# A routed-expert loop on one core: the slot look-up moved between the transposes and the down products, and the residual added in mid-loop

## The reference

```python
comb = (one_hot(expert_id, 32) * weight[..., None]).sum(1)   # top 2 experts of each token
out = zeros((256, 1024))
for e in range(32):
    hg, hu = split(t @ w_gate_up[e], 2)                       # w_gate_up[e]: 1024 x 512
    out = out + comb[:, e:e+1] * ((silu(hg) * hu) @ w_down[e]) # w_down[e]: 256 x 1024
x = layer_norm(alpha * x + out, ln2_g, ln2_b)                 # alpha = 2 ** 0.25
```

## Time and profile before

| what | value |
|---|---|
| time, median of 3 runs | 559.55 us (557.23 to 559.96) |
| the profiled execution: its span | 555.2 us (the profile gives no other time of this execution) |
| median less span | 4.35 us |
| TensorE busy | 499.0 us, 90% of the span |
| VectorE, ScalarE busy | 284.6 us, 168.1 us |
| HBM read | 143.60 MB |

### The profile page before, as it was taken

The page is one execution under the profiler, slowest core; times in us unless marked ns, Lnnn a source line. Parts: engine busy times, 40 slices in busy tenths (PEclk is TensorE's granted clock), DMA queues, the critical chain, the costliest instruction groups (busy, mean ns, idle before and its releaser), DMA issues.

```text
span 555.2 us, 7508 instructions
## 1 busy us (share of the span) xinstructions
PE 499.0 (90%) x2754; PEld 345.5 (62%) x2754; DVE 284.6 (51%) x559; ACT 168.1 (30%) x332; POOL 24.1 (4%) x39
## 2 busy tenths in 40 slices
PE   5999999998999998999559899999999999999981
PEld 4999999987999895887456364333333333333430
DVE  2489898597789996664745122122222222222116
ACT  3432322457554438343322121111111111111111
POOL 2000000000000000000000001000011111111000
PEclk9999999999999999999757999999999999999996
DMA  7668874424244442357911685999999999999802
GB/s 288 228 266 317 335 269 152 152 76 152 92 175 148 156 152 77 113 168 307 421 50 67 250 344 192 421 418 420 421 423 423 421 422 421 422 423 421 368 1 77
DMA packets 26365, 145.05 MB, mean 261 GB/s; under 512 B 3040, under 2 KB 3296, under 8 KB 13792
## 3 DMA queue, kind: packets, MB, share of 16 engines
q1 hardware_dynamic: 26336, 144.66, 67.0%
HBM read 143.60 MB, written 1.05 MB: 261 GB/s over the span
## 4 chain that ended last, share of the span: by engine, by line
PE 76%; DVE 15%; ACT 5%; issue 2%; DMA 1%; ACTq 0%; SPq 0%; DVEq 0%
PE bank L1258 20%; PE bank L1277 11%; PE bank L1067 10%; PE bank L1045 7%; PE bank L1047 6%; PE bank L1046 6%; DVE slots L679 5%; PE bank L1290 3%; DVE w_lo L665 3%; PE bank L1291 3%; PE bank L1233 2%; ACT w_hi L438 1%; PE bank L1188 1%; PE bank L1109 1%; ACT kT L599 1%
## 5 line engine op out<-in xcount | busy, mean ns | idle before, releaser
L1258 PE MATMUL bank<-slots,raw 128*64 128x512 f32 x496 | 113.4, 595 | 0.0
L679 DVE SCALAR_TENSOR_TENSOR slots<-slots,par 128x256 f32<-128x256 f32 x240 | 98.3, 477 | 0.2
L1045 PE MATMUL bank<-x_hi,w_hi 128*128 128x256 f32 x304 | 90.4, 297 | 7.7 <-DVE w_lo L665 4.8
L1046 PE MATMUL bank<-x_lo,w_hi 128*128 128x256 f32 x304 | 86.0, 283 | 0.0
L1047 PE MATMUL bank<-x_hi,w_lo 128*128 128x256 f32 x304 | 85.9, 283 | 0.0
L665 DVE TENSOR_TENSOR w_lo<-raw,w_hi 128x1024 fp32r<-128x1024 f32 x54 | 66.0, 1222 | 38.5 <-ACT w_hi L438 38.5
L438 ACT CAST w_hi<-raw 128x1024 fp32r<-128x1024 f32 x54 | 56.6, 1047 | 57.7 <-PE bank L1047 51.3
L1067 PE MATMUL bank<-gates,raw 128*128 128x256 f32 x288 | 67.9, 391 | 6.7 <-DMA raw<-in_w_in 6.7
L1258 PEld LDWEIGHTS bank<-slots,raw 128*64 128x64 f32 x496 | 35.2, 137 | 60.7 <-issue 60.3
L1277 PE MATMUL bank<-slots,kT 128*64 128x512 f32 x256 | 58.5, 598 | 12.0 <-ACT kT L599 12.0
L983 DVE SCALAR_TENSOR_TENSOR pT<-pT,kT,bank 128x256 f32<-128x256 f32 x16 | 7.7, 480 | 112.2 <-ACT pT L593 112.2
(11 more groups left out here) (181 smaller groups left out, 542.2 us busy)
## 6 DMA issues: line engine op xcount, KB each, us to landing
slots<-in_w_gate_up SPq DMA_DIRECT2D x62, 1024.0 KB, 12.5
slots<-in_w_down SPq DMA_DIRECT2D x32, 1024.0 KB, 14.3
raw<-in_w_in SPq DMA_DIRECT2D x48, 512.0 KB, 4.5
raw<-in_w_attn SPq DMA_DIRECT2D x8, 512.0 KB, 3.4
raw<-in_w_conv SPq DMA_DIRECT2D x8, 512.0 KB, 3.4
raw<-in_w_out SPq DMA_DIRECT2D x8, 512.0 KB, 3.4
spare<-in_w_gate_up SPq DMA_DIRECT2D x2, 1024.0 KB, 11.5
gates<-in_xT SPq DMA_DIRECT2D x2, 512.0 KB, 5.4
```

Of the source, the lines that this page charges most:

```text
L679: ins = nc.vector.scalar_tensor_tensor(acc[:, i, :], h_pad[:, i, tap:tap + SEQ], w, acc[:, i, :], ALU.mult, ALU.add)
L1045: mm(dst, ah, bh, start=first, stop=False, **kw)
L1046: mm(dst, ah, bl, start=False, stop=False, **kw)
L1258: ins = mm(gu_bank[j * WIN:(j + 1) * WIN, :], xg[u][:, k, j * WIN:(j + 1) * WIN], w, start=(k == 0), stop=(k == KT - 1))
```

## The change

The look-up for the next pair stands between the transposes and the down products, and writes into `gu_bank` (bank 0) for every pair but the first. `gate_up` now waits until ScalarE has copied token and weight out of that bank. The look-up does not wait for `hT_copied` any more. ScalarE copies token and weight ahead of `split_y_hi`. The loop of TensorE is cut in two (pairs 4 to 7 and pairs 8 to 13), with `residual` between them in place of its old position in the last pair.

```diff
+        def info_bank(p):
+
+            return turn_bank if is_pair(p, 0) else gu_bank
@@ copy_info, ScalarE
-                nc.scalar.copy(token[u], turn_bank[:, 0:1])
+                nc.scalar.copy(token[u], info_bank(p)[:, 0:1])
                 for j in range(2):
                     ins = nc.scalar.copy(weight[u][j * WIN:(j + 1) * WIN, :],
-                                         turn_bank[j * WIN:(j + 1) * WIN, 1 + j:2 + j])
+                                         info_bank(p)[j * WIN:(j + 1) * WIN, 1 + j:2 + j])
@@ pair, ScalarE
                 copy_hT(p)
-                split_y_hi(p)
                 if not last:
                     copy_info(p + 1, 1 - u)
+                split_y_hi(p)
@@ slot_info, TensorE
                 pe.wait_ge(gat_built, p + 1)
-                if from_pair(p, 1):
-                    pe.wait_ge(hT_copied, p)
                 for t in range(TT):
-                    ins = mm(turn_bank[:, 0:3], gat[u][:, t, :], info[u][:, t, :], start=(t == 0), stop=(t == TT - 1))
+                    ins = mm(info_bank(p)[:, 0:3], gat[u][:, t, :], info[u][:, t, :], start=(t == 0), stop=(t == TT - 1))
@@ gate_up, TensorE
                     pe.wait_ge(h_ready, p)
+                    pe.wait_ge(info_copied, p + 1)
@@ pair, TensorE
                 if last:
-                    residual(first=False)
                     scatter(p - 1, 1 - u)
...
                 turn_h(p)
+                if not last:
+                    slot_info(p + 1, 1 - u)
                 for j in range(2):
                     pe.wait_ge(wd_loaded[2 * u + j], 16 * turn)
                 down(p, (2 * u, 2 * u + 1))
-                if not last:
-                    slot_info(p + 1, 1 - u)
@@ the loop, TensorE
-            with pe.Fori(2, PAIRS // 2 - 1) as i:
+            with pe.Fori(2, PAIRS // 4) as i:
+                for u in range(2):
+                    pair(i * 2 + u, u, i + 1)
+            residual(first=False)
+            with pe.Fori(PAIRS // 4, PAIRS // 2 - 1) as i:
                 for u in range(2):
                     pair(i * 2 + u, u, i + 1)
```

## The result

The changed kernel took 548.82 us (median of 4 runs, 548.18 to 549.83) against 559.33 us for the kernel before (4 runs, 557.23 to 559.96). The ratio is 0.983, with a 95% interval from 0.9805 to 0.9855. The forecast was 552.6 us, with a range down to 550.8.

A forecast was written before the change was run, and what follows sets the result against it. TensorE's order was taken to bound the loop, with the weights close behind. Look-up -8.1 + 0.3, residual 0, lost cover +0.75 and weights +0.15 gave -6.9 us: 559.55 to 552.6 us, range 550.8 to 556.5.

The forecast's parts named there:

- The bound: Expert loop: TensorE's order sets the time; the weights' lead is down to 2.6 us at pair 14.
- The look-up: Gap between transposes and down products hides it: 15 times 0.54 leave the chain, -8.1 us, with +0.3 us remaining.
- The residual: Moved from ahead of pair 15 to between pairs 7 and 8: -3.54 and +3.54 us; the queue does not run dry.
- The lost cover: Tail, `scatter(14)`: the split behind `down(14)` is no longer covered by the residual, 2.6 - 1.85 = +0.75 us.
- The weights: Landings come 1.04 us earlier; `gate_up(14)` waits 0.14 us for its third piece, written +0.15, bounds 0 and 1.2.
- The sum: All terms of the change together: -6.9 us, made against the span of 555.2, which becomes 548.3.
- From span to median: Outside the span: the median lies 4.35 us above it and nothing there changes, so 559.55 - 6.9 = 552.65 us.
- A: `gate_up(14)`: weights set the time, landings do not move forward, wait 1.2 us, 553.7 us in all; chance 0.14.
- B: Gap before down products does not hide the look-up: 556.2 us if half hidden, 560.3 if not at all; chance 0.11.
- C: Entry of TensorE's second loop: instruction fetch queues behind the weights, 11.1 us, giving 563.7 us, slower; chance 0.05.

The follow-up runs named there:

- The look-up alone: Changed kernel with the residual put back ahead of pair 15, so only the look-up moves, against the kernel before: 553.68 us, ratio 0.9929.
- its lighter version: Look-up moved, residual ahead of pair 15, only an eighth of each expert's down weights loaded from pair 2 on, against the kernel before: 547.49 us, ratio 0.9811.

## Why the prediction was right and wrong

**The bound.** Right. TensorE's order set the loop, and the weights were met at pair 14, as said, as the only wait. The look-up alone and its lighter version show both halves of that.

**The look-up.** Right in kind, too small in size. From `gate_up(0)` to `gate_up(15)` the steps of the two traces, less the residual, the uncovered split and the wait, are 9.85 us shorter for 15 look-ups, 0.66 each, where the sum had 0.52. The gap did hide it: it grew in two pairs only, by 0.03 us in pair 6 and 0.16 in pair 7, and in the trace of the look-up alone it did not grow in these two. The sum had allowed 0.3 for this. The rest comes from `gate_up`, which is 0.15 us shorter directly behind the down products than behind the look-up, 13 times over (15 x 0.54 + 13 x 0.15 - 0.2 = 9.85). In the changed kernel it is again 7.02 behind the residual. Down and gate products use half the columns of the array each (64), and look-up, residual and scatter all 128, so a change of shape seems to cost 0.15 us. The first weight loads of `gate_up` in the trace of after speak for it, behind the down products and behind the residual:

```profile
391.00 0.15 PEld L1261 LDWEIGHTS bank<-slots,raw 128*64 128x64 f32 x2 [0.28 <-issue]
...
422.47 0.20 PEld L1261 LDWEIGHTS bank<-slots,raw 128*64 128x64 f32 x4 [0.76 <-issue]
```

In the first place the loads start 0.60 us ahead of the products at 391.60, and in the second only 0.07 ahead of those at 422.54, so there the load is not covered by the products before it. No run changed the shape alone, so the cause stays argued.

**The residual.** Right. It took 3.63 us in mid-loop and 3.54 in the tail. The lost cover is 2.58 us from the end of `down(14)` to `gate_up(15)`, against 1.85 for the scatter before: 0.73, forecast 0.75.

**The weights.** The wait was sized 0.15 and is 1.03 us, since TensorE came earlier than thought. Measured from `gate_up(0)` on, the third piece of pair 14 lands 2.2 us earlier than before, not 1.04. Of that 1.39 is the earlier issue at 344.21. The other 0.8 us I cannot place.

**The sum.** -9.85 + 0.09 + 0.73 + 1.03 = -8.0 us inside the expert part, against -6.9. `gate_up(0)` started 0.76 us later in the one trace of after, and 0.1 more lies behind `gate_up(15)`. So the span came out 7.1 us shorter, at nearly the predicted value, by luck: the loop gained 1.1 more, and the trace of after began 0.76 later. Inside the 1.1 two misses go against each other as well, the look-ups with 2.05 us more gain and the wait for weights with 0.88 more loss.

**From span to median.** This is the step that failed: "The median of the runs lies 4.35 above the span, and nothing in what lies around the span changes". A run lies 1.7 to 1.9 us above its own span. The 4.35 compared the span of one execution with the time of another. The profiled execution, at 555.2, belongs to a time near 557, the shorter group. Two of the three runs shown lie at 559.55 and 559.96, the longer group, and so does the median. What the longer group adds was taken for a constant and carried over, which put the forecast about 2.6 us too high. That alone takes it to 550.0 us, already outside the range, whose bounds had no term for it. The other 1.1 us down to the measured 548.82 are the loop's greater gain. The four first runs of the changed kernel all fell into its shorter group, and the difference of the medians became 10.5 us. On a chip where both kernels were run in turn the changed kernel takes 7.3 us less (549.1 to 551.0 us by the interval). The -6.9 of the sum lies inside that, but within either group the difference is 7.6 to 7.7, nearer to the -8.0 of the traces. Why one set of runs falls mostly into one group stays open.

**The rivals.** By the sign that the prediction named, a wait of over 1 us, A would be called right: `gate_up(14)` is 1.03 us longer (the row of the wait has 0.9). A gave the right place of the wait, but its premise, landings that do not move, is wrong: they moved by 2.2 us. So that sign did not tell A from the forecast. B falls by the gap in the trace. C falls: at `gate_up(8)`, the entry of the second loop, there is no gap, and the 0.16 us ahead of `down(7)` are missing in the second trace of the changed kernel. The Trainium skill's rule on taken branches ("Runtime: NRT & Kernel Launch", section "Instruction fetch mechanics") shows no cost at this entry in this trace. The signs by which the prediction was to fail, a pair over 14 us or a span over 552, both stayed away: none of them looked at the step from span to median.

## What to carry to other kernels

Small work that TensorE does between large products is free in a gap in which TensorE waits for another engine's copy, if it reads nothing that the copy makes and is over before the copy and its hand-over are. Where TensorE's order and the weights run close together, filler work belongs ahead of the point at which the weights are met, since behind it the same work is paid in full. Before a span is turned into a time, each run's own span has to be set beside its time, and if the runs fall into groups, the forecast has to say from which group it starts.

## What the runs showed of the hardware that I had not expected

- The granted clock made two groups of runs of one and the same kernel, 2.3 us apart in the traces. In the longer group it fell once more at 312 us (0.59 over the next 3 us), which cost 1.3 us, after TensorE had been busy 1.15 of 3 us. In another trace TensorE was busy 1.06 of those 3 us and the clock did not fall.
- The clock differed ahead of that too: it rose from its half level between 299 and 302 us early or late (0.96 or 0.70 over that stretch), and from 126 to 130 us it was at 1.00 in one trace and at 0.59 and 0.55 in another, which cost 1.5 us.
- Two look-ups in a row (8 passes of 3 columns) take 0.79 us behind the transposes, where one adds 0.34. One behind the down products takes 0.54.
- `gate_up` takes 6.87 us behind products that use 64 columns of the array and 7.02 behind products that use 128.
- 30 products whose result nobody reads, in TensorE's idle time, brought the next stage forward: it starts at 298.20 and 297.73 in the two traces with them, and at 300.75 to 302.34 in the others.
